# Attention B with transposed scores, row maxima from a single-pass product, and gates kept in DRAM

## The reference

```
z   = rms_norm(x) @ w_in                  # A: q,k,v | B: c_q, c_kv, k_rope | gate_A, gate_B
q   = (rms_norm(c_q) @ w_uq)              # B: 8 heads of 96 (64 + 32 rotary)
k,v = (rms_norm(c_kv) @ w_ukv)            # B: 64 of k (+ shared k_rope) and 64 of v a head
q,k = rms_norm(q), rms_norm(k), rotary on the last 32
s   = (q @ k.T) * 96 ** -0.5, -inf where chunk(key) > chunk(query)      # chunks of 64
y_B = softmax(s) @ v
m   = sigmoid(gate_A) * (y_A @ W_branch_A) + sigmoid(gate_B) * (y_B @ W_branch_B)
x   = x + m @ W_out
x   = x + relu(rms_norm(x) @ W_ff1) ** 2 @ W_ff2
```

## Time and profile before

| | |
|---|---|
| time, median of 3 runs | 1513.15 us (1512.38 to 1515.72) |
| the profiled execution, its own time | 1513.11 us |
| its span, first to last instruction | 1511.0 us |
| TensorE busy | 1446.1 us (96%) |
| VectorE, ScalarE, GpSimd busy | 646.2 (43%), 337.5 (22%), 508.4 us (34%) |
| mean granted TensorE clock | 0.985 |
| chain of waits | TensorE 88%, VectorE 5%, issue 3% |
| data moved | 70.9 MB, mean 47 GB/s |

### The profile page before, as it was taken

How to read it: one execution, slowest core, us unless ns; L and a number is a source line. 1 busy time by engine, 2 the same in 40 slices (tenths; PEclk the granted TensorE clock), 3 DMA queues, 4 the chain that set the end, 5 groups by cost and what they waited for, 6 DMA issues and landing times.

```text
span 1511.0 us, 18576 instructions
## 1 busy us (share of the span) xinstructions
PE 1446.1 (96%) x7304; PEld 1208.7 (80%) x7304; DVE 646.2 (43%) x1038; ACT 337.5 (22%) x717; POOL 508.4 (34%) x351
## 2 busy tenths in 40 slices
PE   7999999977799999999989999999999999999998
PEld 6998888855588877888878787887878788787887
DVE  5300124078566665554247425253442525344242
ACT  5112120175455554200032101010110101011010
POOL 3231554127144240145316134150523406052320
PEclk9999999998899999999999999999999999999999
DMA  7120212000010000015202112030211203021012
GB/s 226 31 57 15 56 42 55 3 21 1 18 38 2 1 8 23 28 43 184 65 6 78 42 38 74 1 97 14 69 42 30 81 0 97 14 66 45 28 42 97
DMA packets 79285, 70.90 MB, mean 47 GB/s; under 512 B 7808, under 2 KB 70784, under 8 KB 79232
## 3 DMA queue, kind: packets, MB, share of 16 engines
q1 hardware_dynamic: 79088, 69.67, 15.3%
q10 hardware_dynamic: 144, 0.52, 0.1%
HBM read 65.99 MB, written 4.19 MB: 46 GB/s over the span
## 4 chain that ended last, share of the span: by engine, by line
PE 88%; DVE 5%; issue 3%; ACT 2%; POOL 1%; DMA 1%; SPq 0%; DVEq 0%; ACTq 0%; POOLq 0%
PE PS L982 73%; PE PS L1175 4%; PE PS L1129 4%; PE PS L989 2%; PE PS L1091 1%; PE PS L1148 1%; DVE relu_sq L1620 1%; ACT scA L891 1%; PE PS L1093 1%; POOL scA L681 1%; PE PS L1155 1%; PE PS L1171 1%; DVE x_norm L1580 0%; DVE scA L1479 0%; DMA x_in<-in_x 0%
## 5 line engine op out<-in xcount | busy, mean ns | idle before, releaser
L571 POOL TENSOR_SCALAR w_hi<-raw 128x1024 fp32r<-128x1024 f32 x64 | 74.2, 1159 | 419.4 <-PE PS L982 409.7
L1620 DVE TENSOR_TENSOR relu_sq<-relu_t 128x512 f32<-128x512 f32 x64 | 118.1, 1884 | 172.6 <-ACT relu_t L960 172.6
L1632 DVE TENSOR_TENSOR xr<-PS,xr 128x1024 f32<-128x1024 f32 x64 | 78.4, 1225 | 245.0 <-PE PS L982 245.0
L573 POOL TENSOR_TENSOR w_lo<-raw,w_hi 128x1024 fp32r<-128x1024 f32 x64 | 168.3, 2629 | 5.3
L982 PE MATMUL PS<-w_hi,uT_hi 128*128 128x512 f32 x512 | 158.4, 391 | 8.1 <-DVE uT_lo L1626 8.1
L982 PE MATMUL PS<-h2T_hi,w_hi 128*128 128x512 f32 x512 | 159.0, 389 | 0.0
L982 PE MATMUL PS<-h2T_lo,w_hi 128*128 128x512 f32 x512 | 158.9, 389 | 0.0
L982 PE MATMUL PS<-h2T_hi,w_lo 128*128 128x512 f32 x512 | 158.9, 389 | 0.0
L982 PE MATMUL PS<-w_lo,uT_hi 128*128 128x512 f32 x512 | 157.7, 389 | 0.0
L982 PE MATMUL PS<-w_hi,uT_lo 128*128 128x512 f32 x512 | 157.6, 389 | 0.0
L960 ACT ACTIVATE relu_t<-PS 128x512 f32<-128x512 f32 x64 | 34.8, 596 | 504.4 <-PE PS L982 504.4
(11 more groups left out here) (194 smaller groups left out, 2430.6 us busy)
## 6 DMA issues: line engine op xcount, KB each, us to landing
raw<-in_w_ff SPq DMA_DIRECT2D x64, 512.0 KB, 3.8
g_raw<-in_w_in SPq DMA_DIRECT2D x16, 512.0 KB, 3.9
x_in<-in_x SPq DMA_DIRECT2D x8, 512.0 KB, 10.7
raw<-in_w_out SPq DMA_DIRECT2D x8, 512.0 KB, 3.6
xr<-in_x SPq DMA_DIRECT2D x8, 512.0 KB, 8.0
out<-xr SPq DMA_DIRECT2D x8, 512.0 KB, 2.6
z_raw<-in_w_in SPq DMA_DIRECT2D x4, 640.0 KB, 8.1
z_raw<-in_w_in SPq DMA_DIRECT2D x4, 544.0 KB, 3.6
```

What stands on the lines that cost most here:

```text
L571: pool.tensor_scalar(hi_ap, raw_ap, 1.0, 1.0, ALU.mult, ALU.mult).then_inc(hi_done, 1)
L573: pool.tensor_tensor(lo_ap, raw_ap, hi_ap, ALU.subtract).then_inc(ready, 1)
L1620: dve.tensor_tensor(relu_sq[:, cols], relu_t[:, cols], relu_t[:, cols], ALU.mult).then_inc(relu_sq_ready, 1)
L1632: dve.tensor_tensor(xr[:, t, :], pair(4 + 2 * (t % 2)), xr[:, t, :], ALU.add).then_inc(x3_added, 1)
```

## The change

Attention B is turned around. Scores are made with keys in rows and 512 queries in columns, so that the exponential is already what the value product needs, and no probabilities are transposed. Since a row maximum then no longer lies in a row, it is taken ahead from a single-pass product of the high parts (`approx`), in the old orientation, by VectorE (`row_max`), negated, and moved from its column by DMA into row 96 of `qT_hi` (`nmax_move`); `kT_hi` has ones in that row, so that the contraction over 97 rows subtracts it. q and k of four heads are kept as high and low parts; the low ones are made by VectorE behind ScalarE's high ones. The scores are three single-pass products.

A head has 12 slots: four key blocks for queries 0 to 511, eight for queries 512 to 1023 (`slot`). TensorE's order of a slot t is scores(t), the next head's row-maximum product (in slots 4 to 11), preparations, values(t-2). `vB` has a column of ones, so y comes with its sum as 65 rows. ScalarE copies it out (`y_out`), and three moves in the SP queue bring the sum to a column, the reciprocals to DRAM and back as rows (`sum_move`, `reciprocal_spread`); VectorE multiplies, ScalarE and VectorE make the high and low parts of `yT`. The transposes of `yB` go. The preparations of group 1 lie in head 0, two in a slot (`FIRST`), those of groups 2 and 3 in heads 1 and 2, 3 and 4, eight a head (`EVEN`).

The gates: each tile is stored to DRAM from two buffers, and fetched again, four tiles after the last scores, the rest behind the last reciprocal. Weights of group 1 are loaded at once. GpSimd splits A's part of yT between preparations; branch A of the first two tiles is computed ahead of branch B's.

```diff
-        gate = place("gate", 88, [P, 2 * KD, S])
+        gate = [place(f"gate{i}", 88 + 4 * i, [P, S]) for i in range(2)]
...
+        def slot(t):
+            h, r = t // HEAD_SLOTS, t % HEAD_SLOTS
+            half, kt = (0, r) if r < Q_BLOCK else (1, r - Q_BLOCK)
+            return h, half, kt, P * max(0, kt - Q_BLOCK * half)
...
+        EVEN = (0, 1, 2, 3, 4, 6, 8, 10)
+        FIRST = (0, 0, 1, 1, 2, 2, 3, 3, 7, 7, 8, 8, 10, 10, 11, 11)
+        def preparations(t):
+            h, r = t // HEAD_SLOTS, t % HEAD_SLOTS
+            if h == 0:
+                return [(1, p) for p in range(2 * T) if FIRST[p] == r]
+            if h > 2 * (B_GROUPS - 2):
+                return []
+            g = (h + 3) // 2
+            return [(g, (0 if h % 2 else T) + p) for p in range(T) if EVEN[p] == r]
...
+            for u in range(4):
+                gate_load(u)
+            for u in range(2 * KD):
+                sp.wait_ge(gate_ready, u + 1)
+                sp.dma_start(gate_d[u], gate[u % 2][:, :]).then_inc(gate_stored[u % 2], 16)
+                if u + 4 < 2 * KD:
+                    gate_load(u + 4)
...
+            def nmax_move(u):
+                h, half = u // 2, u % 2
+                with nc.allow_non_contiguous_dma(reason="128 numbers from a column to a row"):
+                    for i in range(Q_BLOCK):
+                        n = Q_BLOCK * half + i
+                        sp.wait_ge(nmax_ready, Q_BLOCK * u + i + 1)
+                        sp.dma_start(qT_hi[h % KQ_RING][QK:QK + 1, n * P:(n + 1) * P].bitcast(F32), b_nmax[:, u % 2, i:i + 1]
+                                     ).then_inc(nmax_landed[u % 2], 16)
...
+            def sum_move(u):
+                sp.wait_ge(y_raw_ready, u + 1)
+                sp.dma_start(b_sum[:, u % 2, :], sum_row(u).rearrange("o (p t) -> o p t", t=Q_BLOCK)
+                             ).then_inc(sum_landed[u % 2], 16)
+            def reciprocal_spread(u):
+                s, r = u % 2, V_DIM * ((u // 2) % 2)
+                sp.wait_ge(rsum_b_ready, u + 1)
+                sp.dma_start(r_d[s], b_rsum[:, s, :]).then_inc(r_stored, 16)
+                sp.wait_ge(r_stored, 16 * (u + 1))
+                sp.dma_start(r_row[s][r:r + V_DIM, :],
+                             r_d[s].rearrange("p t -> (p t)").rearrange("(o q) -> o q", o=1).partition_broadcast(V_DIM)
+                             ).then_inc(r_landed[s], 16)
...
+            for h in range(B_HEADS):
+                if h < 2:
+                    sp.wait_ge(proj_done, T * (h + 1))
+                    group_load(h + 2)
+                if h == 1:
+                    sp.wait_ge(pv_done, N_A)
+                    branch_load(0)
+                    branch_load(1)
+                sum_move(2 * h)
+                if h + 1 < B_HEADS:
+                    nmax_move(2 * h + 2)
+                reciprocal_spread(2 * h)
+                if h + 1 < B_HEADS:
+                    nmax_move(2 * h + 3)
+                else:
+                    for b in range(2):
+                        sp.wait_ge(gate_stored[b], 16 * KD)
+                    sp.wait_ge(st_done, N_SLOTS)
+                    gate_fetch(0)
+                    gate_fetch(1)
+                sum_move(2 * h + 1)
+                reciprocal_spread(2 * h + 1)
+            for d in range(2, KD):
+                gate_fetch(d)
+                branch_load(d)
...
+            def exp_b(t):
+                h, half, kt, c0 = slot(t)
+                act.wait_ge(st_done, t + 1)
+                if t == 0:
+                    act.wait_ge(pv_done, N_A)
+                if t >= P_RING:
+                    act.wait_ge(slot_done, t - P_RING + 1)
+                p, sc = prB[t % P_RING], PS[:, 2 + t % S_RING, :]
+                if kt >= Q_BLOCK * half:
+                    act.activation(p[0:CHUNK, c0:c0 + CHUNK], sc[0:CHUNK, c0:c0 + CHUNK], ACT.Exp)
+                    act.activation(p[:, c0 + CHUNK:HALF], sc[:, c0 + CHUNK:HALF], ACT.Exp).then_inc(p_ready, 1)
                 else:
+                    act.activation(p[:, :], sc, ACT.Exp).then_inc(p_ready, 1)
...
+            def y_out(u):
+                odd = (u // 2) % 2
+                act.wait_ge(slot_done, block_end(u))
+                if u >= 2:
+                    act.wait_ge(yB_ready, u - 1)
+                dst, src = y_raw[u % 2], PS[:, 5 + u % 2, :]
+                if odd:
+                    act.activation(dst[0:1, :], src[V_DIM:V_DIM + 1, :], ACT.Copy)
+                    act.activation(dst[V_DIM:P, :], src[0:V_DIM, :], ACT.Copy).then_inc(y_raw_ready, 1)
+                else:
+                    act.activation(dst[0:V_DIM + 1, :], src[0:V_DIM + 1, :], ACT.Copy).then_inc(y_raw_ready, 1)
+            def y_high(u):
+                h, half = u // 2, u % 2
+                rows, cols = slice(V_DIM * (h % 2), V_DIM * (h % 2) + V_DIM), slice(half * HALF, (half + 1) * HALF)
+                act.wait_ge(y_normed, u + 1)
+                act.activation(yT_hi[4 + h // 2][rows, cols], y_raw[u % 2][rows, :], ACT.Copy).then_inc(yB_hi_done, 1)
+            for t in range(N_SLOTS):
+                exp_b(t)
+                for g, p in preparations(t):
+                    group_act(g, p)
+                for u in range(BLOCKS):
+                    if t == block_end(u) + 2:
+                        y_out(u)
+                    if t == block_end(u) + 7:
+                        y_high(u)
...
+            def approx(a):
+                h, n = a // T, a % T
+                q, k = qT_hi[h % KQ_RING], kT_hi[h % KQ_RING]
+                if a == 0:
+                    pe.wait_ge(max_ready, N_A)
+                if n == 0 and h % B_GROUP == 0:
+                    pe.wait_ge(qk_ready, T * (h // B_GROUP + 1))
+                if n == 0 or n >= 4:
+                    if a:
+                        pe.wait_ge(nmax_ready, a)
+                elif a > 1:
+                    pe.wait_ge(nmax_ready, a - 1)
+                for c in range(0, (n + 1) * P, 512):
+                    w = min(512, (n + 1) * P - c)
+                    out = PS[:, n % 2, 0:w] if n < 4 else PS[:, c // 512, 0:w]
+                    ins = pe.matmul(out, q[0:QK, n * P:(n + 1) * P], k[0:QK, c:c + w], start=True, stop=True)
+                ins.then_inc(approx_done, 1)
...
+            def scores_t(t):
+                h, half, kt, c0 = slot(t)
+                s = h % KQ_RING
+                keys, cols = slice(kt * P, (kt + 1) * P), slice(half * HALF + c0, (half + 1) * HALF)
+                if t == 0:
+                    pe.wait_ge(max_ready, N_A)
+                    pe.wait_ge(pt0_ready, N_A)
+                    pe.wait_ge(k_one_ready, KQ_RING)
+                if kt == 0:
+                    u = 2 * h + half
+                    pe.wait_ge(nmax_landed[u % 2], 16 * Q_BLOCK * (u // 2 + 1))
+                if t >= S_RING:
+                    pe.wait_ge(p_ready, t - S_RING + 1)
+                out = PS[:, 2 + t % S_RING, c0:HALF]
+                pe.matmul(out, kT_hi[s][0:QK + 1, keys], qT_hi[s][0:QK + 1, cols], start=True, stop=False)
+                pe.matmul(out, kT_hi[s][0:QK, keys], qT_lo[s][0:QK, cols], start=False, stop=False)
+                pe.matmul(out, kT_lo[s][0:QK, keys], qT_hi[s][0:QK, cols], start=False, stop=True
+                          ).then_inc(st_done, 1)
...
+            def values_t(t):
+                h, half, kt, c0 = slot(t)
+                u, g = 2 * h + half, h // B_GROUP
+                last = t + 1 == block_end(u)
+                pe.wait_ge(p_ready, t + 1)
+                if kt == 0 and u >= 2:
+                    pe.wait_ge(y_raw_ready, u - 1)
+                if t % (2 * HEAD_SLOTS) == 0 and g < 3:
+                    pe.wait_ge(v_one_ready, g + 1)
+                if t == 0:
+                    pe.wait_ge(y_ready, N_A)
+                out = PS[0:V_DIM + 1, 5 + u % 2, :]
+                v, p = vB[g % 3][:, kt, h % B_GROUP, :], prB[t % P_RING]
+                if kt >= Q_BLOCK * half:
+                    pe.matmul(out[:, c0 + CHUNK:HALF], v, p[:, c0 + CHUNK:HALF], start=kt == 0, stop=False)
+                    ins = pe.matmul(out[:, c0:c0 + CHUNK], v[0:CHUNK, :], p[0:CHUNK, c0:c0 + CHUNK], start=False,
+                                    stop=last)
                 else:
+                    ins = pe.matmul(out, v, p[:, :], start=kt == 0, stop=False)
+                ins.then_inc(slot_done, 1)
...
+            for t in range(N_SLOTS):
+                scores_t(t)
+                for a in approx_at(t):
+                    approx(a)
+                for g, p in preparations(t):
+                    group_step(g, p)
+                if t >= 2:
+                    values_t(t - 2)
...
+            pe.wait_ge(yA_split, 4)
+            for d in range(2):
+                pe.wait_ge(bw_ready, d + 1)
+                if d == 0:
+                    pe.wait_ge(nmax_ready, T * B_HEADS)
+                    pe.wait_ge(p_ready, N_SLOTS)
+                else:
```

(32 more changed lines are left out.)

631 lines of the change are left out of this document (281 added, 350 removed).

## The result

The changed kernel takes 1566.38 us (median of 4 runs, 1563.89 to 1572.07) against 1514.43 for the kernel before beside it: ratio 1.0357, interval 1.0336 to 1.0378, so 52 us slower. The prediction had the sign, and its size too small: 1529.4, with 1546 as the upper end. The profiled execution took 1565.74, span 1563.7, where the one of before had 1511.0.

A forecast was written before the change was run, and what follows sets the result against it. TensorE's own work was taken to bound attention B. Start +2.3, work -14.2, losses +29.9 and tail -1.7 gave +16.3 us on 1513.15, so 1529.4; forecast range 1518 to 1538 (chance 0.52), wider range 1508 to 1546.

The forecast's parts named there:

- What bounds the kernel now: Attention B before the change: bounded by TensorE's own work, with TensorE busy 52.26 of 52.5 us, then 103.02 of 103.3.
- TensorE's work, 176.1: Attention B: TensorE has 176.1 us of work left after the change against 190.3 before, so 14.2 us less.
- narrow products: Attention B: single-pass products of 128 and 256 columns cost f32 prices, 26 us at worst, halfway 1542; chance 0.10.
- costly low-order passes: Attention B's scores: low-order passes as dear as f32, 23 us a head instead of 6.5; held excluded, no chance given.
- Start of attention A, 4.3: Start of attention A: 2.7 us later for the last gate's store and 1.6 for VectorE's four rows of ones.
- (a) Pairs, 18.5: Head 0 of attention B: 18.5 us of waits, 13.2 of them from eight pairs of preparations sharing bank 7.
- (b) Chains, 15.8: Attention B, heads 1 to 7: 15.8 us of waits, from three-move chains, late maxima, preparations and GpSimd.
- the bound with slow moves, 22: Attention B, heads 1 to 7: with 2.6 us a move, the predicted waits grow from 15.8 to 22 us.
- (c) Clock, 6: Head 0 of attention B, about 60% busy: 6 us lost to half-clock work, range 2 to 12.
- the prediction's own sign of being wrong: Attention B: a granted clock under 0.9 from head 1 on would show the forecast wrong; so would two other signs.
- the rival: All of attention B at a granted clock of 0.87: 20 us more than the 6 taken, 1549; chance 0.15.
- Tail, 5.4: Behind attention B: a 3.4 us gap for the last chain plus 2.0 for a low clock on restart, 7.1 before.

The follow-up runs named there:

- zeroed corners: Changed kernel with the masked 64 x 64 corner of each diagonal probability block written as zeros by ScalarE, one 128-row value product replacing two: 1568.55 us, ratio 1.0361.
- the execution that lost 13.0: Changed kernel with the two value products of a diagonal block in the other order, corner product first; a single run, 1558.61 us.

## Why the prediction was right in sign and too small

The predicted end of attention B was 620.3 and is 654.5. Step by step:

- **What bounds the kernel now**: right for the kernel before.
- **TensorE's work, 176.1**: failed by 20.7. The single-pass prices were right (0.23, 0.17, 0.12, 0.11), so the rivals on narrow products and on costly low-order passes fall. The mis-sized term is the diagonal value products: the forecast took 0.22 for a 64-row product and nothing for its neighbours. A half head's diagonal took 3.14 in place of 2.71, and the score products behind it 0.4 more: 0.83 x 16 = 13.3 us. Of the other 7 us about 4 are in the kernel before too: to 602.3 us its work is 194.4 where the forecast's sum had 190.3. The trace shows where such time lies, not all of it. Head 7, which never waits, takes 18.3 us where these prices, with the corners' 0.83, give 18.2. In head 6, 0.7 us over, it lies at row-maximum products: the pass at 626.89 is followed after 2.10 us with 1.70 of them counted as idle, so 0.40 go for a pass of 0.23. The first part of a wait counts as busy time, because the length of the last product reaches into it; a kernel with more waits shows more "work". The Trainium skill (TensorEngine Tiling (Array Packing), "Key Properties") says that a change of tiling mode drains TensorE. The trace agrees, if that is what a 64-row product is: about 0.1 us on each side of it, in either order of the pair. No run shows the mechanism itself.
- **Start of attention A, 4.3**: too small by 1.2. The store's part is 2.25 (2.7 forecast; 2.5 came back when the load went first). The memsets are 0.91 us each and not 0.69, and hold VectorE 3.26 us (1.6 forecast). Together 5.5, and the last value products of attention A do come 5.3 to 5.8 us later (396.98 and 397.52 before, 402.27 and 403.29 now). Row maximum 3 ends at 403.23, its move takes the forecast's 2.1 or so, and attention B starts at 405.44, 2.0 later than forecast. No run left the memsets out.
- **(a) Pairs, 18.5**: right. Head 0 is idle 17.1 us; the eight second preparations wait 1.41 to 2.43 us, 13.2 together, which is the forecast's 13.2. It lasted 59.5, not 48.2 (29.7 + 18.5): 4.4 more work, 8.3 of clock, 1.4 less idle.
- **(b) Chains, 15.8**: it looks right, since heads 1 to 7 are idle 13.9 us, but it was a sum made for less work. The nearest kernel with the forecast's work is the one with zeroed corners (177.1 against 176.1), though with more work for ScalarE, and there heads 1 to 7 are idle 32.2 us: 5.2, 5.8, 6.5, 6.4, 3.7, 3.9 and 0.7, against 3.5, 2.6, 3.5, 1.9, 1.9, 1.9 and 0.5. Head 0 is at 18.3, as forecast. For that kernel (b) would be half its size, and the bound with slow moves, 22, too low as well. A part can be in the moves, below: 7.4 us a chain instead of the 6.4 of the sum (2.1 + 1.9 + 2.4), two chains a head, 2 us, which is about what heads 5 and 6 are over by. In the heads with preparations the rest, up to 2.5 us a head, was not told apart.
- **(c) Clock, 6**: failed by 15.4. It cost 21.4: 8.3 in head 0, 4.8 in head 1, 8.5 in head 4, whose clocks of 0.87 and 0.74 in heads 1 and 4 are the prediction's own sign of being wrong (under 0.9 from head 1 on). Head 4 has less idle time than heads 2 and 3, but behind a wait of 1.19 us at 566.81 TensorE ran some 17 us at half speed though busy all the time; why there and not in heads 2 and 3 is open. The reason given against the rival, that stretches with 1.2 us waits kept 0.99, came from a piece in which such waits were few. The rival had the mechanism, and with 20 more than the 6 it was nearer (15.4 measured, 7.0 in the execution that lost 13.0).
- **Tail, 5.4**: measured 7.5, of which the gap is 4.3 (3.4 forecast).

The moves' row, by DMA issues of the changed kernel in attention B (KB each, median us to landing):

```profile
r_row<-r_store SPq DMA_DIRECT2D x15, 128.0 KB, 3.1
...
b_sum<-y_raw SPq DMA_DIRECT2D x16, 2.0 KB, 2.0
r_store<-b_rsum SPq DMA_DIRECT2D x15, 2.0 KB, 2.3
```

The forecast had set the fixed part of a store at 1.0 from a large one, and had said that the trace did not agree with the 2 us of the Trainium skill (DMA: Bandwidth & Descriptors, "Anatomy of one DMA"). A small store takes 2.3. That is near the page's figure, which the page gives for moves that GpSimd issues, while these are SyncE's; the inference from a 512 KB store was wrong.

Term by term the misses add up: 2.0 (start) + 20.7 (work) + 15.4 (clock) - 3.8 (idle) + 2.1 (tail) = 36.4, and 1529.4 + 36.4 = 1565.8. By the sum, then, two steps failed: the price of the diagonal value products, and the term for the clock, 6 us where a TensorE that waits 31 us lost 21.4.

But the sum misleads about causes. In the run with the corners the work is as forecast and the time no better: there the misses are 1.6 (start) + 1.0 (work) + 15.5 (clock) + 15.7 (idle) + 5.9 (behind attention B), which gives 1569.1, and its profiled execution took 1569.0. So a third step failed, the one that added work and waits as if they were independent: work saved on TensorE turned into waits for the other engines, and a TensorE that waits that much does not keep its clock. That VectorE's and ScalarE's queues were counted too short is the likely reason; how much of it the corners' own operations on ScalarE add is not settled. The wrong price of the 64-row products would then have fallen for the most part into idle time: its removal was worth nothing alone, and 6.8 us once other waits were gone.

## What to carry to other kernels

When a rewrite saves work on the engine that bounds a stage and adds round trips, ask first whether that engine still bounds it: here 19.7 us less work on TensorE, bought with 16 us more on ScalarE, were worth nothing, and 6.8 once other waits were gone. Spreading work that shares one buffer cost no work and gave more than any saving (18.9 us); the order of two entries of a queue gave 4.7. And where TensorE waits often, add the clock: here it cost 21.4 us on 31.0 of idle time, and 13.0 on 32.4 in another execution.

## What the hardware showed that I had not expected

- Doing needless work made the kernel 9.4 us faster by the median: with 10 us of products in TensorE's waits the profiled execution lost 10.0 us to half speed, where those without lost 21.4 and 13.0.
- The granted clock is a matter of chance near such waits. Runs of one kernel spread by up to 17 us (1548.24 to 1565.19), with mean clocks of 0.977 and 0.965; the kernel before, which hardly waits in attention B, spreads by up to 8.8 us in 13 runs (1508.51 to 1517.30).
- A product on 64 rows among products on 96 to 128 costs about 0.1 us on each side.
- Four memsets of one row of 1024 on one partition cost VectorE 0.91 us each, more than the 0.69 of a cast over 128 partitions.
- VectorE's reciprocal takes 3337 ns for 1x512, 6.5 ns an element, and 0.17 us for 128x4.
